# A block inversion by one product and one transpose a level, and expert slots in two blocks of 88 rows

## The reference

```python
kb = kc * bc[..., None]
A = jnp.where(strict, jnp.einsum("bhncd,bhnsd->bhncs", kb, kc) * decay, 0.0)
rhs = jnp.concatenate([vc * bc[..., None], kb * jnp.exp(gc)[..., None]], axis=-1)
sol = lax.linalg.triangular_solve(A, rhs, left_side=True, lower=True, unit_diagonal=True)
u, w = sol[..., :Dv], sol[..., Dv:]
```

```python
def expert_block(args):
    xb, e = args
    return (jax.nn.silu(xb @ w_gate[e]) * (xb @ w_up[e])) @ w_down[e]
out = jnp.zeros((n, d), h.dtype).at[row_tok].add(yb * row_w[:, None].astype(yb.dtype))
```

## Time and profile before

| | |
|---|---|
| median of 3 runs | 4768.59 us (4755.41 to 4770.2) |
| the profiled execution | 4758.82 us, its span 4757.0 us |
| mean granted clock of PE | 0.892 |
| PE busy | 4208.0 us, 88% |
| PEld busy | 3488.0 us, 73% |
| DVE busy | 1832.0 us, 39% |
| ACT busy | 1226.5 us, 26% |
| POOL busy | 165.1 us, 3% |

### The profile page before, as it was taken

The page is one execution under the profiler, slowest core; times in us unless marked ns, Lnnn a source line. Parts: engine busy times, 40 slices in busy tenths (PEclk is TensorE's granted clock), DMA queues, the critical chain, the costliest instruction groups (busy, mean ns, idle before and its releaser), DMA issues. The chain is left out here.

```text
span 4757.0 us, 58198 instructions
## 1 busy us (share of the span) xinstructions
PE 4208.0 (88%) x22504; PEld 3488.0 (73%) x22504; DVE 1832.0 (39%) x3297; ACT 1226.5 (26%) x2114; POOL 165.1 (3%) x136
## 2 busy tenths in 40 slices
PE   7998888997998888899786787999878879999998
PEld 5777776775777777677475665787655679999997
DVE  2366644233246663523326554332244421111112
ACT  2463223231256222323132112222223311111101
POOL 0240000000032000000000000000000000000000
PEclk9988778998998777899897788999986789999999
DMA  3000001221200000222120001231220024444343
GB/s 121 32 1 1 0 36 71 89 89 51 95 7 1 1 0 36 88 89 88 53 75 1 0 1 73 84 104 67 94 81 0 18 100 169 158 180 159 145 150 124
DMA packets 51456, 324.56 MB, mean 68 GB/s; under 512 B 6528, under 2 KB 7424, under 8 KB 20352
## 3 DMA queue, kind: packets, MB, share of 16 engines
q1 hardware_dynamic: 51328, 322.85, 18.9%
HBM read 319.68 MB, written 2.10 MB: 68 GB/s over the span
## 5 line engine op out<-in xcount | busy, mean ns | idle before, releaser
L490 PE MATMUL bank<-high 128*128 128x512 f32 x2480 | 981.5, 396 | 116.3 <-DVE low L584 81.4
L491 PE MATMUL bank<-low,high 128*128 128x512 f32 x2480 | 977.8, 394 | 0.0
L492 PE MATMUL bank<-high,low 128*128 128x512 f32 x2480 | 976.0, 394 | 0.0
L490 PEld LDWEIGHTS bank<-high 128*128 128x128 f32 x2480 | 473.2, 191 | 224.7 <-issue 67.6
L492 PEld LDWEIGHTS bank<-high,low 128*128 128x128 f32 x2480 | 473.3, 191 | 100.1
L491 PEld LDWEIGHTS bank<-low,high 128*128 128x128 f32 x2480 | 474.0, 191 | 98.6
L548 DVE TENSOR_TENSOR low<-weight_ring,high 128x2048 fp32r<-128x2048 f32 (+1 forms) x144 | 319.3, 2218 | 554.7 <-ACT high L505 554.7
L2851 PE MATMUL bank<-chosen,glu_ring 128*128 128x176 f32 x2816 | 422.2, 313 | 0.0
L2851 PEld LDWEIGHTS bank<-chosen,glu_ring 128*128 128x128 f32 x2816 | 420.0, 190 | 0.1
L505 ACT ACTIVATE high<-weight_ring 128x2048 fp32r<-128x2048 f32 (+1 forms) x144 | 266.5, 1852 | 269.1 <-PE bank L492 230.2
L2862 PE MATMUL bank<-hidden,down_ring 128*128 128x176 f32 x1408 | 211.3, 313 | 0.0
(11 more groups left out here) (464 smaller groups left out, 5169.7 us busy)
## 6 DMA issues: line engine op xcount, KB each, us to landing
glu_ring<-in_w_expert SPq DMA_DIRECT2D x88, 1024.0 KB, 4.9
weight_ring<-in_w_ff SPq DMA_DIRECT2D x64, 1024.0 KB, 4.9
down_ring<-in_w_expert_down SPq DMA_DIRECT2D x64, 704.0 KB, 5.1
weight_ring<-in_w_in SPq DMA_DIRECT2D x22, 1024.0 KB, 4.9
weight_ring<-in_w_ffe SPq DMA_DIRECT2D x22, 1024.0 KB, 4.8
weight_ring<-in_w_downe SPq DMA_DIRECT2D x16, 704.0 KB, 4.1
weight_ring<-in_w_ino SPq DMA_DIRECT2D x11, 1024.0 KB, 4.8
weight_ring<-in_w_ine SPq DMA_DIRECT2D x9, 1024.0 KB, 4.8
```

The lines of the kernel that those rows point to most:

```text
L490: nc.tensor.matmul(mem.bank[b][:, :], whole, high[:, k, :], start=(k == 0), stop=False)
L491: nc.tensor.matmul(mem.bank[b][:, :], whole, low[:, k, :], start=False, stop=False)
L492: last = nc.tensor.matmul(mem.bank[b][:, :], rest, high[:, k, :], start=False, stop=(k == kt - 1))
```

## The change

`invert` keeps one matrix, which now has the identity on its diagonal from the start. In each level PE transposes it (`turn`, one `nc.tensor.transpose` for each chunk, L1410), DVE masks the transpose out of PSUM into `joint` (the mask now has the diagonal too), PE multiplies (`clear`, L1417, one product of 128 columns for each chunk, L1419 in the last level), and ACT copies the product over the matrix (L1380). The final result is twice the inverse, so the copies of what is solved with it get a factor 0.5. What ACT did beside it in one go is dealt out, one piece behind each copy. The identity is added in `delta_prepare` by POOL and in `rwkv_prepare` by DVE. In the expert jobs the slots stand in two blocks of 88 rows, and the products with the identity are transposes.

```diff
-        def _(dve):
-            def join(n, l):
-                mask = mem.levels[:, upper[n], l, :].unsqueeze(1).broadcast_to([P, TT, P])
-                nc.vector.tensor_tensor(chunks(joint[:, n, :]), chunks(turned[:, n, :]), mask, ALU.mult) \
-                    .then_inc(joined[n], 1)
...
-                    nc.vector.tensor_tensor(at, at, of_side(mem.bank[2 * n][:, :], l, n), ALU.add).then_inc(added[n], 1)
-                    if not last_level:
-                        nc.vector.tensor_tensor(neg[:, n, :], neg[:, n, :], mem.bank[2 * n + 1][:, :], ALU.add) \
-                            .then_inc(added[n], 1)
-                        dve.wait_ge(added[n], 2 * l + 2)
-                        join(n, l + 1)
+        @block.scalar
+        def _(act):
+            for l in range(last_level):
+                for n in range(count):
+                    act.wait_ge(product[n], l + 1)
+                    nc.scalar.activation(matrix[:, n, :], mem.bank[2 * n][:, :], ACT.Copy).then_inc(taken[n], 1)
+                    if beside is not None:
+                        beside.scalar(l, n, rows_exped)
...
         def _(dve):
             for l in range(LEVELS):
                 for n in range(count):
+                    dve.wait_ge(turned[n], l + 1)
+                    mask = mem.levels[:, upper[n], l, :].unsqueeze(1).broadcast_to([P, TT, P])
+                    nc.vector.tensor_tensor(chunks(joint[:, n, :]), chunks(mem.bank[2 * n + 1][:, :]), mask, ALU.mult) \
+                        .then_inc(joined[n], 1)
                 if late is not None and l < late.groups:
                     dve.wait_ge(late_product, l + 1)
                     late.take(l).then_inc(late_taken, 1)
+            for n in range(count):
+                dve.wait_ge(product[n], LEVELS)
+                nc.vector.tensor_tensor(chunks(twice[:, n, :]), chunks(mem.bank[2 * n][:, :]), idents, ALU.add)
...
+            def turn(l, n):
+                if l >= 1:
+                    pe.wait_ge(taken[n], l)
+                for c in slices:
+                    last = nc.tensor.transpose(mem.bank[2 * n + 1][:, c], matrix[:, n, c], ident)
+                last.then_inc(turned[n], 1)
+
+            def clear(l, n):
+                pe.wait_ge(joined[n], l + 1)
+                for c in slices:
+                    if l < last_level:
+                        last = nc.tensor.matmul(mem.bank[2 * n][:, c], joint[:, n, c], matrix[:, n, c], start=True, stop=True)
+                    else:
+                        last = nc.tensor.matmul(mem.bank[2 * n][:, c], matrix[:, n, c], joint[:, n, c], start=True, stop=True)
+                last.then_inc(product[n], 1)
+
             for n in range(count):
+                turn(0, n)
+            lag = count // 2
             for l in range(LEVELS):
                 for n in range(count):
+                    clear(l, n)
+                    if n >= lag and l < last_level:
+                        turn(l + 1, n - lag)
+                    elif n < lag and 1 <= l and count > 2:
+                        turn(l, n + count - lag)
                 if late is not None and l < late.groups:
                     if l >= late.banks:
                         pe.wait_ge(late_taken, l - late.banks + 1)
                     late.multiply(l).then_inc(late_product, 1)
+                if count == 2 and l < last_level:
+                    turn(l + 1, 1)
...
+        @block.gpsimd
+        def _(pool):
+            for n in range(len(streams)):
+                pool.wait_ge(neg_made, TT * (n + 1))
+                chunks = b.neg[:, n, :].rearrange("p (t c) -> p t c", t=TT)
+                nc.gpsimd.tensor_tensor(chunks, chunks,
+                                        CONST(mem.const, "ident").unsqueeze(1).broadcast_to([P, TT, P]), ALU.add)
...
-    heights = [min(P, BLOCK - s * P) for s in range(BLOCK_TILES)]
+    height = BLOCK // BLOCK_TILES
+    parts = [slice(s * height, (s + 1) * height) for s in range(BLOCK_TILES)]
...
-                        last = nc.tensor.matmul(high[half * BLOCK_TILES + s][0:heights[s], c * P:(c + 1) * P],
-                                                result[:, half * KD // 2 + c, s * P:s * P + heights[s]],
-                                                CONST(mem.const, "ident"), start=True, stop=True)
+                        last = nc.tensor.transpose(high[half * BLOCK_TILES + s][0:height, c * P:(c + 1) * P],
+                                                   result[:, half * KD // 2 + c, parts[s]], CONST(mem.const, "ident"))
...
-                        nc.tensor.matmul(high[s][0:heights[s], t * P:(t + 1) * P], picks[:, t, slots],
-                                         CONST(mem.const, "ident"), start=True, stop=True)
+                        nc.tensor.transpose(high[s][0:height, t * P:(t + 1) * P], picks[:, t, parts[s]],
+                                            CONST(mem.const, "ident"))
```

More of the change, by code:

```diff
@@ L84 @@
 BLOCK_TILES = -(-BLOCK // P)
+assert BLOCK % BLOCK_TILES == 0
 MAX_JOBS = N_EXPERTS + (SEQ * TOP_K - N_EXPERTS) // BLOCK
@@ L1328, in scalar @@
                 .then_inc(rows_exped, 1)
[L1329 to L1333, removed]
+        elif level <= 3:
+            kind, to, rows_of = ((G_BETA, b.vb, b.v_rows), (G_BEXP, b.kb, b.k_rows), (G_KDEC, b.kd, b.k_rows))[level - 1]
+            for t in range(TT):
+                nc.scalar.activation(to[:, n, t, :], rows_of[:, t, self.lanes[par]], ACT.Copy,
+                                     scale=b.cols[:, kind * TT + t, d, par:par + 1])
+        elif level == 4:
             nc.scalar.activation(b.last_decay[self.lanes[par], d, :],
@@ L1340, in gpsimd, with invert @@
             self.nc.gpsimd.tensor_tensor(self.b.qg[:, d, :], self.b.qg[:, d, :], self.b.q[:, :], ALU.mult)
-def invert(nc, mem, neg, turned, upper, late=None, beside=None):
+def invert(nc, mem, matrix, twice, upper, late=None, beside=None):
     count = len(upper)
-    def of_side(columns, level, n):
-        return columns.rearrange("p (g h b) -> p g h b", h=2, b=2 ** level)[:, :, 0 if upper[n] else 1, :]
     def chunks(x):
@@ L1411, in _ @@
+            def clear(l, n):
[6 more added lines that the diff above has]
+                last.then_inc(product[n], 1)
             for n in range(count):
-                for c in slices:
-                    last = nc.tensor.matmul(mem.bank[2 * n][:, c], neg[:, n, c], CONST(mem.const, "ident"),
-                                            start=True, stop=True)
@@ L1579, in delta_net @@
             delta_prepare(nc, mem, u, cols, rows, hp, b)
-            invert(nc, mem, b.neg, b.turned, [0, 0, 1, 1], beside=ScanInputs(nc, rows, hp, b))
+            invert(nc, mem, b.neg, b.twice, [0, 0, 1, 1], beside=ScanInputs(nc, rows, hp, b))
             delta_scan(nc, mem, y, hp, b)
@@ L1848, in _ @@
             steps.settle()
+            for par in range(2):
+                steps.did(nc.vector.tensor_tensor(by_chunk(b.neg[:, par, :]), by_chunk(b.neg[:, par, :]),
+                                                  CONST(mem.const, "ident").unsqueeze(1).broadcast_to([P, TT, P]), ALU.add))
+            steps.settle()
         @block.scalar
@@ L2080, in time_mix @@
         rwkv_prepare(nc, mem, vec, u, decay, rate, j, b, products)
-        invert(nc, mem, b.neg, b.turned, [0, 0], products)
+        invert(nc, mem, b.neg, b.twice, [0, 0], products)
         rwkv_scan(nc, mem, y, j, b)
@@ L2879, in job @@
                         for part, rows in enumerate((rows_high, rows_low)):
-                            last = nc.tensor.matmul(low[k % EXP_SLOTS][:, :], rows[0:heights[s], s, k * P:(k + 1) * P],
-                                                    spreader[0:heights[s], s, :], start=(s == 0 and part == 0),
+                            last = nc.tensor.matmul(low[k % EXP_SLOTS][:, :], rows[0:height, s, k * P:(k + 1) * P],
+                                                    spreader[0:height, s, :], start=(s == 0 and part == 0),
                                                     stop=(s == BLOCK_TILES - 1 and part == 1))
```

81 lines of the change are left out of this document (29 added, 52 removed).

## The result

| kernel | median | ratio to the kernel before |
|---|---|---|
| before, 4 runs beside the changed kernel | 4762.69 us (4755.41 to 4770.2) | |
| changed, 4 runs | 4620.99 us (4616.4 to 4631.79) | 0.9706 [0.9679, 0.9732] |

What follows compares the result with a forecast made beforehand. PE was taken as the bound in all three stretches. 4758.8 - 71 (delta inversions) - 11 (time mix) - 21 (expert jobs) = 4656 us for the profiled execution; the median was given as 4660 us, range 4632 to 4705.

Steps and rivals of the forecast that it cites:

- so I set them at zero: Expert jobs: blocks of 88 and 88 rows cost the same as 128 and 48, at most -0.4 to +0.4 us a job.
- The experts' transposes: Expert jobs: transposes for products with the identity save 2.7 us a job, 21 us in eight jobs.
- The delta inversions: Six delta inversions: each falls from 55.3 to 43.4 us, a gain of 71 us.
- the stall of ACT: Delta inversions: ACT falls 3.1 us behind PE, 1.8 us are covered and about 1.4 us reach PE.
- 1.6 us a stream in levels 1 to 3: Delta inversions: ACT's time for a copy and a piece of the scan's inputs, against PE's 1.34 us.
- The cover of 1.8 us: Delta inversions: 2.7 us of other PE work between product and transpose, less 0.9 for the copy, hides ACT's lag.
- The time mix: Four time-mix inversions with `rwkv_prepare`: 2.8 us gained a call, 11 us in all, a level at 4.7 us.
- the saved 0.9 us turns into a wait: Time-mix levels: DVE takes the late group before masking, so PE waits and a level stays at 4.7 us.
- Preparation: Preparation: POOL's identity additions set at zero; rival that they end after DVE, up to 5 us a call, 4690 us, chance 0.08.
- The clock did not stay at half: Rival for the inversions: clock stays at half throughout, 18 us more per inversion, 4918 us, chance 0.05.
- Handoffs are covered: Delta inversions: other streams' work hides handoffs; rival that it does not, 8.4 us more a call, 4717 us, chance 0.10.
- the change does nothing that shows: Rival for the whole kernel: saved products become waits everywhere, only the experts' 21 us or less stay, chance 0.05.

## Why the prediction was wrong, point by point

**What failed: the expert jobs.** "The blocks of 88 and 88 rows have together the columns of 128 and 48, and the moving sides are as wide, so I set them at zero; they could be -0.4 to +0.4 us a job if a narrow load is not priced by its columns." They were worth 33.0 us, 4.1 a job, ten times the bound that I gave. The step counted columns and asked only if a narrow load is cheaper. It isn't, in that the step was right (184 and 188 ns a load). It never asked what stands between two matmuls: the trace of before had it in front of me, 0.33 us from one spreading matmul to the next, and weight loads idle for 45.4 us ahead of that line with no releaser. What the runs showed in its place is 0.20 us for each change between up to 64 rows and more, and about 0.09 us for each change to or from 48 stationary columns. Even the earlier trace rows held a piece of it: the late group of 64 rows took 1.09 us to the next product where eight instructions take 0.90, and I took the difference for the group's own length. A part that is said to cost nothing has to be looked up like the others.

**The experts' transposes** were forecast at 21 us and measured at 21.0. PE was the bound there and stayed it; DMA is at 0.46.

**The delta inversions** were forecast at 43.4 us each and are 250.6 / 6 = 41.8, 81 us in all where I had 71. 8.4 of the 10 us are the stall of ACT, 1.4 a call, which isn't there: the step that failed is "1.6 us a stream in levels 1 to 3". I added durations of ACT instructions that overlap when they follow each other (1.6 us instead of 1.43). The prices of product and transpose and the clock (0.50 for 5.2 us, then 1.00) were right. The cover of 1.8 us was enough for the 1.2 that ACT falls behind; its size wasn't measured. The doubled copy shows that the stall is real as soon as ACT is slower.

**The time mix.** The mechanism was right, DVE's in-order queue with a wait of "about 1 us" (0.79), the sizes were somewhat off: a level is 4.97 us and not 4.7. About 0.2 of the 0.27 us lie at the change to the late group of 64 rows, which wasn't in the sum (0.203 and 0.213 us between the starts there, where neighbours have 0.11); the change back lies inside PE's wait. The gain with `rwkv_prepare` is 8.3 - 2.4 = 5.9 us where I had 11. I saw that "the saved 0.9 us turns into a wait" and stopped there; moving one instruction of DVE takes it back, 26 us in four calls.

**Preparation.** POOL's additions in the delta calls are hidden: these phases changed by under 0.3 us. In `rwkv_prepare` the two additions (L1856) come last and cost 0.6 us a call (0.5 forecast).

**The rivals.** The clock did not stay at half: 0.50 from 364.3 to 369.5, 1.00 from 369.6 to 407.0 in the first call, and the repeated turnings rule it out for transposes alone. Handoffs are covered, but not by much. The experts' gain was not lost to the weights. That the change does nothing that shows fell with the 142 us; only in the time mix did a saved product turn into a wait.

**The sum** came to 103 us with -71, -11 and -21; measured are -81, -6 and -54. The median of 4660 us doesn't follow from the text ahead of it: 4656 us for the profiled execution and 10 us for the median above it are 4666. It matters little beside the 33 us of the blocks. The clock of stretches behind the inversions had no term either; in the pair of profiled executions it cancelled, in other kernels here it didn't.

## What to carry to other kernels

Count a kernel's matmuls by the rows of their operands, and look at the seams: if a sequence goes back and forth between up to 64 and more rows, split the rows evenly (88 and 88 for 128 and 48), or order them so that equal ones are neighbours. Where a round over several engines gets shorter, read the queue of the engine that is now waited for: an instruction that used to stand behind the urgent one may now stand ahead of it. For a queue of short instructions on one engine take the distance from start to start, not the sum of durations.

## What the runs showed of the hardware

- Between fp32 matmuls with up to 64 rows and ones with more, in either direction, lie about 0.2 us that neighbours of equal kind don't have (12.4 us for 63 changes by the reordered blocks, 3.2 us for 16 by the even ones). The weight load behind such a change starts with its matmul and not 0.22 us ahead of it. 104 beside 72 rows is free, 112 beside 64 isn't, although the weight loads take the same 182 to 191 ns in all of them. The Trainium skill (TensorE: Matmul & The Clock Gate, Part 2, LDWEIGHTS) says that a load doesn't depend on the number of rows; the rows agree, but the price lies in when the load starts, not in how long it takes.
- fp32 products with 48 stationary columns beside ones with 128 lose about 0.09 us at the change (0.205 us and not 0.11); with 88 and 88 nothing is lost.
- With nothing but fp32 transposes on PE the granted clock went from 0.50 (5.1 us, 25 transposes) to 1.00, and one takes 4.20 / 41 = 0.10 us there.
- A stretch of 26.7 us at a granted clock of 0.50 in one kernel was 17.5 us at 0.98 in another with the same instructions. Between kernels that differ only upstream of it a stretch moved by 7 to 10 us in this way, so parts are compared stretch by stretch, and their sum with the median only roughly.
